# Seven block products for eight in 48 of a mixer's 72 input tiles, and all four branch merges behind the last branch

## What is computed

```python
h = rmsnorm(x) * (1 + s_m) + b_m
proj = h @ w_in          # columns for four branches and for four merge gates of 1024 each
y1 = gdn(...); y3 = ssd(...); y2 = rg_lru(...); y0 = s5(...)      # each 512 wide
merged = sum(sigmoid(gate_k) * (y_k @ w_branch_k) for k in range(4))
x = x + g_m * (merged @ w_out)
x = x + g_f * grouped_moe(...)         # 16 experts, two per token
```

## Time and profile before

| | before |
|---|---|
| runs | 2662.4, 2665.77, 2668.4 us |
| profiled execution, span | 2667.6 us |
| TensorE busy (matmul) | 2500.6 us, 94% |
| VectorE / ScalarE / GpSimd busy | 1007.8 / 714.2 / 64.4 us |
| chain that ended last | PE 81%, DMA 8%, DVE 5%, ACT 4% |
| matmuls of whole tiles, L536 | 2544 instructions, 828.4 us busy |
| gate matmuls, L680 | 1920 instructions, 537.0 us busy |
| SP's loads of expert weights | 532, end of the program |

### The profile page before, as it was taken

One profiled execution on the slowest core, in us unless ns is written; L12 is line 12 of the kernel. 1 busy time (PEld: TensorE's weight loads), 2 busy tenths in 40 slices (PEclk: granted clock), 3 DMA queues, 4 the chain that ended last, 5 costly groups with the idle time before them and its releaser, 6 DMA issues.

```text
span 2667.6 us, 39247 instructions
## 1 busy us (share of the span) xinstructions
PE 2500.6 (94%) x16348; PEld 1548.4 (58%) x16348; DVE 1007.8 (38%) x1798; ACT 714.2 (27%) x1283; POOL 64.4 (2%) x66
## 2 busy tenths in 40 slices
PE   5998999999999999999999999999996899989995
PEld 3555889875555566555555556765454444444443
DVE  4356555552133144642432539723245011101115
ACT  3132222221111111121233056631024222222224
POOL 0000000000000000000000000000000000000003
PEclk9999999999999999999999999999998999999997
DMA  7000212213111002231103011131307556667436
GB/s 315 32 32 35 75 48 107 95 38 132 35 46 46 35 30 75 75 125 72 38 12 152 32 38 40 40 116 67 110 24 281 210 209 270 234 235 289 172 129 230
DMA packets 65269, 291.99 MB, mean 109 GB/s; under 512 B 8956, under 2 KB 32068, under 8 KB 44612
## 3 DMA queue, kind: packets, MB, share of 16 engines
q1 hardware_dynamic: 52996, 255.92, 25.4%
q0 software_dynamic: 8928, 22.03, 2.4%
q10 hardware_dynamic: 3168, 11.54, 1.1%
HBM read 694.20 MB, written 56.63 MB: 281 GB/s over the span
## 4 chain that ended last, share of the span: by engine, by line
PE 81%; DMA 8%; DVE 5%; ACT 4%; issue 1%; SPq 1%; POOL 0%; DVEq 0%; ACTq 0%; POOLq 0%
PE psum L536 31%; PE psum L680 16%; PE psum L1561 8%; DMA arena<-in_moe 6%; PE psum L1545 4%; PE psum L1419 4%; PE psum L635 2%; ACT arena L1817 2%; PE psum L1134 2%; PE psum L565 1%; PE psum L1020 1%; PE psum L996 1%; PE psum L1530 1%; PE psum L1122 1%; PE psum L1325 1%
## 5 line engine op out<-in xcount | busy, mean ns | idle before, releaser
L536 PE MATMUL psum<-arena 128*128 128x384 f32 x2544 | 828.4, 488 | 10.9 <-DVEq L335 6.1
L536 PEld LDWEIGHTS psum<-arena 128*128 128x128 f32 x2544 | 483.7, 191 | 353.8 <-issue 12.2
L680 PE MATMUL psum<-arena 128*128 128x384 f32 (+1 forms) x1920 | 537.0, 428 | 6.4 <-ACT arena L694 3.3
L680 PEld LDWEIGHTS psum<-arena 128*128 128x128 f32 x1920 | 341.9, 192 | 158.3 <-issue 9.9
L1561 PE MATMUL psum<-arena 128*32 128x256 f32 x5632 | 325.0, 387 | 33.3 <-DMA arena<-in_moe 32.2
L1561 PEld LDWEIGHTS psum<-arena 128*32 128x32 f32 x5632 | 179.1, 111 | 165.3 <-DMA arena<-in_moe 36.0
L1545 PE MATMUL psum<-arena 128*32 128x512 f32 x1408 | 161.4, 597 | 9.7 <-DMA arena<-in_moe 9.2
L1986 ACT ACTIVATE arena<-psum 32x512 f32<-32x512 f32 x174 | 102.4, 589 | 229.6 <-PE psum L1545 228.1
L1419 PE MATMUL psum<-arena 128*128 128x512 f32 (+1 forms) x384 | 126.0, 487 | 0.3 <-issue 0.3
L694 ACT ACTIVATE arena<-psum 128x384 f32<-128x384 f32 x96 | 46.7, 490 | 294.4 <-PE psum L680 233.9
L2693 DVE TENSOR_TENSOR arena<-arena,psum 128x256 f32<-128x256 f32 x44 | 18.5, 421 | 279.4 <-PE psum L1561 192.1
(11 more groups left out here) (554 smaller groups left out, 2436.6 us busy)
## 6 DMA issues: line engine op xcount, KB each, us to landing
arena<-in_moe SPq DMA_DIRECT2D x532, 1024.0 KB
arena<-in_ada SPq DMA_DIRECT2D x12, 2048.0 KB, 8.9
gate_raw<-arena SPq DMA_DIRECT2D x96, 192.0 KB, 1.8
arena<-gate_raw SPq DMA_DIRECT2D x8, 2304.0 KB, 8.5
y_rows<-arena ACTq DMA_DIRECT2D x22, 512.0 KB, 3.2
arena<-in_gate SPq DMA_DIRECT2D x5, 2048.0 KB, 8.2
arena<-in_br SPq DMA_DIRECT2D x4, 2048.0 KB, 8.0
arena<-in_qkv SPq DMA_DIRECT2D x3, 2048.0 KB, 15.0
```

The source lines that it names most:

```text
L536: last = nc.tensor.matmul(pset(s)[:, n, :], w[:, kk, :], src[:, kk, n * N3:(n + 1) * N3], start=(kk == 0), stop=(kk == K - 1))
L680: last = nc.tensor.matmul(bank(6 + u % 2)[:, cols * p:cols * (p + 1)], w[:, m % 4, kk, :], HT[:, kk, n * N3 + cols * p:n * N3 + cols * (p ...
```

## The change

**Products.** For 48 tiles (`xbc`, `zd`, gates 3, 2 and 0, `xc`, `gc`, `ua`) two tiles make a pair. Its weights are seen as two by two blocks (two tiles x two halves of K, each four blocks of 128), and a half of the tokens (576) as two by two blocks (two halves of K x two stretches of 288). A *unit* is a pair and a half of the tokens. It takes seven products of four matmuls of 288 columns where plain tiles would have eight. Four sums of weight blocks per pair and three differences of input blocks per half are made on GpSimd, and so are the seven additions per unit that put the products together. The 48 units run as one stream (`STREAM`), first alone (units 0 to 11: `xbc`, `zd`), then as filler of the SSD chunks, between the LRU steps, and in S5.

**Banks.** Each product goes to bank 6 or 7 in turn and may start when the product two before it is evicted. ScalarE evicts three of the seven to their place and four to partial buffers, each behind a wait for GpSimd's additions (`u_add`).

**Order.** There is no merge until the last branch: the four merges follow `glu`. Y of the first three branches is saved to DRAM and loaded again, in the place of `HT` and of S5's input. The phases go from 12 to 4. The counts of matmuls placed in the gaps are new, and the LRU steps have units (1, 1, 2, 2) between them with no tile of `gc` in front of `lru_r`.

**Loads.** Four slots of 1 MB in place of two of 2 MB behind the GDN part.

The core of the diff:

```diff
-def plan_loads():
...
+STREAM = [("xbc", 0), ("xbc", 1), ("xbc", 2), ("xbc", 3), ("zd", 0), ("zd", 1),
+          ("gate3", 0), ("gate3", 1), ("gate3", 2), ("gate3", 3), ("gate2", 0), ("gate2", 1),
+          ("xc", 0), ("xc", 1), ("gc", 0), ("gc", 1), ("gate2", 2), ("gate2", 3), ("ua", 0), ("ua", 1),
+          ("gate0", 0), ("gate0", 1), ("gate0", 2), ("gate0", 3)]
+UNITS = [(a, p, h) for a, p in STREAM for h in range(2)]
+YIELDS = 7 * 4
...
-        counts = [("ops", 16 if last else 19)] + ([("b%d" % b, 3) for b in range(NSEQ)] if last else [("next", 4)])
+        counts = [("pre", 14)] if c == 0 else []
+        counts += [("ops", 20 if last else 24)] + ([("b%d" % b, 4) for b in range(NSEQ)] if last else [("next", 5)])
...
+    points.append((("norm", 0), n + 20))
+LRU_UNITS = [UNIT[("gc", 1, 0)], UNIT[("gc", 1, 1)], UNIT[("gate2", 2, 0)], UNIT[("gate2", 3, 0)], UNIT[("ua", 0, 0)]]
...
-        counts = [("uc", 9 if i else 16), ("scan", (27, 32, 32, 34)[i])] + [("y%d" % q, (1, 2, 2, 3)[i]) for q in range(3)]
+        counts = [("uc", (18, 10, 10, 11)[i]), ("scan", (31, 37, 37, 40)[i])] + [("y%d" % q, (1, 2, 2, 3)[i]) for q in range(3)]
...
+        def pe_units(pe, u0, u1):
+            def product(i, w, x):
+                if i < 2:
+                    pe.wait_ge(g_ev, 3 * KD - 1 + i)
+                else:
+                    pe.wait_ge(u_ev, i - 1)
+                for k in range(4):
+                    last = nc.tensor.matmul(bank(6 + i % 2)[:, 0:NQ4], w[:, k, :], x[:, k, :], start=(k == 0), stop=(k == 3))
+                    if k == 3:
+                        last.then_inc(u_fill, 1)
+                    yield
...
+                yield from product(i, w[:, 0, 0:4], lo[:, :, left(h)])
+                yield from product(i + 1, w[:, 0, 4:8], hi[:, :, left(h)])
...
+                yield from product(i + 2, s2, t2)
+                yield from product(i + 3, s1, t1)
...
+                yield from product(i + 4, s3, lo[:, :, right(h)])
...
+                yield from product(i + 5, s4, hi[:, :, right(h)])
+                yield from product(i + 6, w[:, 1, 4:8], t4)
...
+        def act_products(act, i0, i1):
...
+                if j in (1, 2, 4, 5):
+                    if u or j == 5:
+                        act.wait_ge(u_add, 7 * u + {1: -1, 2: -3, 4: 0, 5: 2}[j])
+                    nc.scalar.activation(partial[{1: 0, 2: 1, 4: 2, 5: 0}[j]], src, ACT.Copy).then_inc(u_ev, 1)
+                    continue
+                c = {0: 0, 3: 3, 6: 2}[j]
+                if u in GATE_NO:
+                    act.wait_ge(u_st[{0: 0, 3: 1, 6: 2}[j]], 16 * GATE_NO[u])
...
         @block.gpsimd
         def _(pool):
+            for u in range(len(UNITS)):
+                then = sums(*STREAM[u // 2 + 1]) if u % 2 and u + 1 < len(UNITS) else itertools.repeat(0)
+                e, i = partial, 7 * u
+                pool.wait_ge(u_ev, i + 3)
+                for dst, x in unit_parts(u, 0, e[1]):
+                    last = add(x, dst, x, ALU.add)
+                C.then(last)
+                accumulate(u, 0, e[0])
+                pool.wait_ge(u_ev, i + 4)
...
+                next(then)
+                pool.wait_ge(u_ev, i + 5)
+                C.then(add(e[2], e[1], e[2], ALU.add))
+                accumulate(u, 3, e[2])
+                next(then)
+                pool.wait_ge(u_ev, i + 6)
+                accumulate(u, 1, e[0])
+                next(then)
+                pool.wait_ge(u_ev, i + 7)
+                accumulate(u, 2, e[2])
+                next(then)
...
             for m in range(4):
-                pe_tile(pe, "gc", m, wg[:, m], HT, KD)
                 pe.wait_ge(s_conv, 20 + m + 1)
...
-                fill("lru", m)
-            signal_phase(pe)
-            pe_merge(pe, 2, 9, l_done, 0)
-            end_phase(pe, 10)
+                units(LRU_UNITS[m], LRU_UNITS[m + 1])
+            units(UNIT[("ua", 0, 0)], UNIT[("gate0", 0, 0)])
...
+            for e, k in enumerate(MERGES):
+                if e < 3:
+                    pe.wait_ge(y_in, 16 * (e + 1))
+                else:
+                    pe.wait_ge(a_gs, 4)
+                for m in range(KD):
+                    if m % 4 == 0:
+                        wk = wait_pair(pe, "br%d" % k, m // 4).rearrange("p (m k c) -> p m k c", m=4, k=KM)
+                    pe_tile(pe, "br%d" % k, m, wk[:, m % 4], YM[k], KM)
```

SP at the end of the SSD (unit 22), before it stores that unit's gates:

```diff
+                if u == 22:
+                    sp.wait_ge(d_ss, NC7)
+                    sp.dma_start(A["ssd_p"], dH).then_inc(s_pstate, 16)
+                    sp.wait_ge(s_pstate, 16 * 3)
+                    sp.wait_ge(d_ss, NC7 + NSEQ)
+                    sp.dma_start(A["ssd_s"], W[1]).then_inc(s_pstate, 16)
+                    sp.dma_start(rows[:, 0:1024], A["lru_w"][0][:, 0:1024]).then_inc(s_rest, 16)
+                    sp.wait_ge(s_pstate, 64)
+                    load_pair(sp, "xc", 0)
+                    load_pair(sp, "xc", 1)
+                sp_store_gates(sp, u)
```

More of the change, by code:

```diff
@@ L73, in plan_tiles @@
               ("gdn_sp", 1, 1), ("gdn_sp", 2, 0), ("gdn_sp", 3, 1), ("zb", 3, 0)]
[L74 to L83, removed]
+    names += [("ssd_ss", 0, 1)]
+    names += [x for m in range(4) for x in (("lru_r", m, 0), ("lru_i", m, 1))]
     names += [("glu", m, m % 2) for m in range(4)]
-    names += merge(0)
+    names += [("br%d" % k, m, m % 2) for k in MERGES for m in range(KD)]
     count, at = [0, 0], {}
@@ L92 @@
 FILL = plan_tiles()
-def plan_loads():
[L97 to L112, removed]
+LOADS = [("qkv", 0, 0), ("qkv", 1, 1), ("qkv", 2, 0), ("gate1", 0, 1), ("gate1", 1, 0), ("gdn_state", 0, 1), ("zb", 0, 0)]
+NQ4 = T // 4
+STREAM = [("xbc", 0), ("xbc", 1), ("xbc", 2), ("xbc", 3), ("zd", 0), ("zd", 1),
[3 rows of a table added]
+UNITS = [(a, p, h) for a, p in STREAM for h in range(2)]
+UNIT = {x: u for u, x in enumerate(UNITS)}
+YIELDS = 7 * 4
+GATE_NO = {u: n for n, u in enumerate(u for u, x in enumerate(UNITS) if x[0].startswith("gate"))}
+HALF_LOADS = [(("xbc", 0), 2), (("xbc", 1), 3), (("xbc", 2), 0), (("xbc", 3), 1), (("zd", 0), 2), (("zd", 1), 3),
[5 rows of a table added]
+              (("br0", 0), 2), (("br0", 1), 3), (("out", 0), 0), (("out", 1), 1), (("out", 2), 2), (("out", 3), 3)]
+HALF = {x: (i, sum(j == i for _, j in HALF_LOADS[:n + 1])) for n, (x, i) in enumerate(HALF_LOADS)}
 SLICES = [(640, 512), (128, 512), (0, 128)]
@@ L866, in _, with after_unit @@
[L866 to L879 removed]
+            def after_unit(u):
+                sp.wait_ge(u_fill, 7 * (u + 1))
@@ new lines, in _, with accumulate @@
+            C = Steps(pool, u_add)
+            def accumulate(u, c, x):
+                for dst, part in unit_parts(u, c, x):
+                    last = add(dst, dst, part, ALU.add)
+                C.then(last)
+            for i in range(2):
+                pool.wait_ge(g_st[i], 16 * 12)
+            for _ in sums(*STREAM[0]):
+                pass
+            wait_fill(pool, "zb", 3)
+            for h in range(2):
+                F.then(add(lo[:, :, right(h)], hi[:, :, right(h)], lo[:, :, right(h)], ALU.subtract))
@@ L2525, in _ @@
                     dve_rotation(i + 1)
-            for i in range(2):
-                dve.wait_ge(g_st[i], 16 * 12 * len(MERGES))
+            for i in range(3):
+                dve.wait_ge(u_st[i], 16 * len(GATE_NO))
             for m in range(4):
```

691 lines of the change are left out of this document (375 added, 316 removed), and 5 rows, old and new, of the table HALF_LOADS.

## The result

The changed kernel takes **2703.7 us** (median of 4; 2699.1 to 2704.7), the kernel before 2664.1 (median of 4): ratio 1.014, 95% interval 1.0123 to 1.0157. It is slower by 39.6 us. The forecast was 2679, slower by 13: the sign and the range hold, but the loss is three times as large. The profiled execution has a span of 2702.9 us against the earlier trace rows; 35.3 us are to be explained between the two traces, and 4.3 more because the profiled execution of before stood further above its median than that of the changed kernel.

A forecast was written before the change was run, and what follows sets the result against it. The prediction took TensorE's own work to bound the rewritten stretch. It summed 2667.6 - 91 (work) - 24 (barriers, old waits) + 108 (new waits) + 20 (clock) = 2680.6, less 1.8: about 2679 us, range 2632 to 2712.

The forecast's parts named there:

- TensorE's work, minus 91: In the 48 tiles, seven products per unit replace the plain tiles' matmuls, 652 us for 743: a gain of 91 us.
- Merges at nothing, barriers gone: Four merges after `glu` add nothing at 62.2 us each; old barriers and waits go, minus 24 us.
- New waits, 108: From SSD through S5, two banks cover 3.9 us, not 10.3, so TensorE waits for ScalarE's evictions: plus 108 us.
- chunks and `pre`: Waits in nine SSD chunks, 22 us, and before the first chunk, at ScalarE's SiLU of `zd`, 2.7 us.
- end of the SSD: Waits for ScalarE's squares 8.8 us, a gate store on SP's queue 6, the LRU's constants 3: sum 18 us.
- The clock, plus 20: TensorE runs at a lower clock after waits of 2 us or more: 12 more waits at 1.7 us, plus 20.
- From 1871 us on nothing is touched; I leave it as it is: The experts' part, from 1871 us on, is untouched by the change and was left as it is, with no term.
- The base: The sum started from the old kernel's profiled 2667.6 us and took off 1.8 to reach its median, 2665.8.
- smaller waits: Rival, chance 0.30: ScalarE reaches evictions earlier or few waits are taxed, halving waits and tax; ends between 2615 and 2660.
- In each other's way: Rival, chance 0.20: VectorE and GpSimd exclude each other, 5 us per S5 group, some 25 us in all, 2704.
- longer two-input operations of VectorE: Sign that the forecast is wrong: VectorE's two-input operations grow longer than in the old rows.
- GpSimd the bound: Rival, chance 0.06: above 1.33 us an addition GpSimd paces every unit; at 1.6 us, 132 us more, 2800.

The follow-up runs named there:

- x12: The kernel before, run again with nothing changed: 2665.0 us, ratio 1.0008.
- x7: x3 with SP's gate stores of unit 22 ahead of its wait for the state's store and GELU behind the square root: 2601.0 us, ratio 0.9758.
- x5: The changed kernel run again with nothing altered: 2702.3 us, ratio 1.0135.
- x1: The changed kernel with ScalarE's evictions of the first three products woven into each of the four LRU steps only: 2674.4 us, ratio 1.0045.
- x4: The changed kernel with 13 throwaway matmuls on TensorE in each of the four LRU steps: 2690.6 us, ratio 1.0104.
- x11: The changed kernel with 40 throwaway matmuls between the merges and the last projection: 2702.4 us.
- x2: The changed kernel with GpSimd's seven additions a unit cut to one column, so blocks are not combined: 2693.4 us, ratio 1.0114.
- x3: The changed kernel with ScalarE's evictions woven between its other work everywhere (SSD, LRU, S5): 2616.0 us, ratio 0.9819.

## Why the prediction went as it did

The mechanism was right and the size was not. The steps that failed are two terms of the sum: the clock, taken at 20 us, and the part behind, taken at nothing. The rest of the distance is in the waits and in the trace that the sum started from.

- **TensorE's work, minus 91:** right. An instruction of 288 columns takes 0.2427 us; twelve units alone take 163.3 (13.6 each, as worked out).
- **Merges at nothing, barriers gone:** right: 279.1 us with 278.9 busy. Of the old idle about 4 us were to stay; outside the products there are 8.1.
- **New waits, 108:** right, and by the mechanism named: 108.6 us of idle before products, 108.3 released by ScalarE. That the sums agree to 1 us is luck, since the places are off by -4 to +4 us. By place, forecast and measured: chunks and `pre` 25 and 20.8; end of the SSD 18 and 15.3 (8.5 and 6.8; the gate store I put between them at 6 held ScalarE 2.3 us and TensorE not at all, and the wait for the constants, at 3, took 6.8); LRU 28 and 31.8; S5's constants 5 and 6.1; S5's groups 32 and 33.1 (28.8, and 4.3 in waits of about 1 us between the Y products).
- **The clock, plus 20: too small.** With the work at minus 91, a busy time 61.6 us lower means 29.4 (35.1 against the busy time of x12, 1243.2). In x7, at a clock of 1.00, the products take 30.9 us less than in the changed kernel. The failing numbers are the 1.7 us a wait, taken from one wait of 2.41 us, where those of 6 to 10 us cost 1.7 to 3.3, and counting only some of them: of 16 waits of 2.3 us and more before products, 15 were taxed, by 35 us together, and the one at 1031.44 (2.41 us) was not.
- **"From 1871 us on nothing is touched; I leave it as it is": failed.** It took 8.7 us more, and 807.1 us in x5. Nothing in the change does that by itself (x1, x4 and x11 have the same program there and 794.6 to 796.4 us); what the traces show in place of nothing is 6.1 us more busy time for the same instructions and 2.6 us more idle, with more long waits for the experts' loads and low pace behind most of them. Why this kernel has more of them stays open. The range should have had plus or minus 10 for it: over the kernels that compute everything it ran from 794.6 to 807.1.
- **The base.** I summed against a profiled execution of 2667.6 and took off 1.8. The kernel before in x12 had a part of 1269.65 in place of 1277.35 and a span of 2660.3. The median of its four runs makes the distance 4.3 us longer than the two traces do.
- Together: 13 forecast, plus 4.3 (idle), 9.4 (clock), 8.7 (behind), 4.3 (base): 39.7, measured 39.6.
- **Rival "smaller waits"** fell: ScalarE did not run ahead. **"In each other's way"** was right as a mechanism (VectorE's busy time up by 89 us) and wrong as a place: I put 5 us on each S5 group, and x2 gives 7 us in all, of which 2.9 are not VectorE's, and 0.4 in S5. The prediction had named longer two-input operations of VectorE as a sign that it was wrong. They came (1.36 to between 1.60 and 2.02 us), and yet the loss is not theirs: the sign was badly chosen, as busy time off the path costs little. **"GpSimd the bound"** fell: 0.69 to 1.03 us an addition, under the 1.33 worked out (its price in the prediction, 2800, should have read 2811: 2679 + 132). It is near all the same: once, in an LRU step, the GELU waited 6.5 us for it in x3.

## What to carry to other kernels

In this kernel a filler's worth was set by how long its PSUM banks keep TensorE busy while the evicting engine is elsewhere. Halving the accumulation per bank (16 matmuls ahead became 8, of 288 columns) set 108 us of waits and some 30 of low clock against 91 us of saved work. Before such a change, list the evicting engine's longest stretches without an eviction and spread evictions among them; here that cost nothing but order, and with the stores and the GELU moved it turned plus 39.6 into minus 63. Price every new idle of the lengths seen here with the clock's tax behind it, and give parts that wait on DMA a range of their own even where nothing in them is touched.

## What was not expected of the hardware

- The tax is nearly whole behind a short idle: 0.3 us over the pace behind 1.3 us of idle (no more than any stretch of products has at its end), 1.9 to 2.0 behind 2.3 to 2.8, 1.7 to 3.3 behind 6 to 10. It is not sure: one idle of 2.41 us before products cost nothing. The Trainium skill (TensorE: Matmul & The Clock Gate, Part 1: The HAM clock gate) says that the array's ungated state must be earned by activity; by that rule, the trace agrees, and x4 shows that throwaway matmuls earn it as well.
- GpSimd needs 2.62 us for a 128x1152 addition, 0.69 to 1.03 for 288 columns and, in x2, 0.19 for one column in the median (0.34 in the mean of the largest group).
- VectorE's smallest operations suffer most beside GpSimd: 8 columns 0.17 to 0.64 us, a 3-column copy 0.17 to 0.94 (0.72 with the additions cut short).
- The same program behind the start of the last projection ran 807.1 us in x5 and 794.6 in x11, where it starts 9.6 us later.
